# The squared decay of a gated recurrence, moved from a product on Pool to an exponential on ACT

## The reference, cut to what matters

```python
r = sigmoid(xb @ w_a + b_a)                     # (tokens, 1536)
ig = sigmoid(xb @ w_x + b_x)
log_a = -8.0 * r * softplus(-lam)               # lam: one value for each of the 1536 channels
a = exp(log_a)
bt = sqrt(-expm1(2.0 * log_a)) * (ig * xc)
hs = linear_scan(a, bt)                         # h_t = a_t * h_(t-1) + bt_t
y = hs * silu(g)
return y @ w_out                                # 1536 -> 1024
```

## Time and profile before

| | |
|---|---|
| median of 3 runs | 1854.46 us (1852.45 to 1854.9) |
| the profiled execution | 1852.57 us |
| its span, first to last instruction | 1850.8 us |
| PE busy | 1824.0 us, 99% of the span |
| DVE busy | 1047.5 us, 57% |
| ACT busy | 761.0 us, 41% |
| POOL busy | 208.9 us, 11% |
| recurrent layer with its output projection | from 1597.6 us on |

### The profile page before, as it was taken

How to read it: one execution, slowest core, us unless ns; L and a number is a source line. 1 busy time by engine, 2 the same in 40 slices (tenths; PEclk the granted TensorE clock), 3 DMA queues, 4 the chain that set the end, 5 groups by cost and what they waited for, 6 DMA issues and landing times.

```text
span 1850.8 us, 22596 instructions
## 1 busy us (share of the span) xinstructions
PE 1824.0 (99%) x8210; PEld 1461.3 (79%) x8210; DVE 1047.5 (57%) x1270; ACT 761.0 (41%) x1059; POOL 208.9 (11%) x175
## 2 busy tenths in 40 slices
PE   7999999999999999999999999999999999999997
PEld 5888888888766788888888878787787878788876
DVE  6444443343666665444443347766475566869973
ACT  5333332323544544333233345354343443456662
POOL 3000001011000002000001110100201102213343
PEclk9999999999999999999999999999999999999998
DMA  3232333344321132323223333232222222232333
GB/s 141 91 102 91 102 95 109 102 145 132 98 75 46 58 103 92 102 91 102 92 101 102 102 97 116 74 98 91 80 87 78 92 91 69 91 97 98 103 118 110
DMA packets 50304, 178.60 MB, mean 97 GB/s; under 512 B 5880, under 2 KB 6136, under 8 KB 50240
## 3 DMA queue, kind: packets, MB, share of 16 engines
q1 hardware_dynamic: 46512, 167.27, 27.6%
q0 software_dynamic: 2352, 8.15, 1.5%
q10 hardware_dynamic: 1376, 2.30, 0.3%
HBM read 173.48 MB, written 2.11 MB: 95 GB/s over the span
## 4 chain that ended last, share of the span: by engine, by line
PE 95%; DVE 2%; ACT 2%; POOL 1%; issue 1%; DMA 0%; POOLq 0%; ACTq 0%; DVEq 0%
PE banks L494 28%; PE banks L496 28%; PE banks L495 27%; PE banks L797 2%; PE banks L634 1%; PE banks L684 1%; PE banks L617 1%; PE banks L760 1%; PE banks L780 1%; PE banks L782 1%; PE banks L781 1%; DVE u_lo L1535 1%; ACT w_hi L1006 1%; DVE w_lo L1518 1%; POOL sumsq L2216 1%
## 5 line engine op out<-in xcount | busy, mean ns | idle before, releaser
L1518 DVE TENSOR_TENSOR w_lo<-w_raw,w_hi 128x1024 fp32r<-128x1024 f32 x315 | 403.2, 1280 | 593.2 <-ACT w_hi L1006 592.5
L494 PE MATMUL banks<-u_hi,w_hi 128*128 128x512 f32 x1528 | 607.4, 397 | 15.7 <-DVE u_lo L1535 15.6
L496 PE MATMUL banks<-u_hi,w_lo 128*128 128x512 f32 x1528 | 596.0, 390 | 0.0
L495 PE MATMUL banks<-u_lo,w_hi 128*128 128x512 f32 x1528 | 595.7, 390 | 0.0
L1006 ACT ACTIVATE w_hi<-w_raw 128x1024 fp32r<-128x1024 f32 x315 | 333.3, 1058 | 596.6 <-PE banks L496 551.4
L494 PEld LDWEIGHTS banks<-u_hi,w_hi 128*128 128x128 f32 x1528 | 287.2, 188 | 95.1 <-issue 16.5
L496 PEld LDWEIGHTS banks<-u_hi,w_lo 128*128 128x128 f32 x1528 | 287.4, 188 | 61.3
L495 PEld LDWEIGHTS banks<-u_lo,w_hi 128*128 128x128 f32 x1528 | 287.6, 188 | 60.8 <-issue 3.1
L495 PE MATMUL banks<-hid_lo,w_hi 128*128 128x512 f32 x352 | 136.9, 389 | 0.0
L496 PE MATMUL banks<-hid_hi,w_lo 128*128 128x512 f32 x352 | 136.9, 389 | 0.0
L494 PE MATMUL banks<-hid_hi,w_hi 128*128 128x512 f32 x352 | 136.9, 389 | 0.0
(11 more groups left out here) (290 smaller groups left out, 2329.3 us busy)
## 6 DMA issues: line engine op xcount, KB each, us to landing
w_raw<-weights SPq DMA_DIRECT2D x315, 512.0 KB, 3.5
bias<-neighbour_bias POOLq DMA_DIRECT2D x8, 384.0 KB, 4.9
x<-x_t ACTq DMA_DIRECT2D x4, 512.0 KB, 7.5
v_win<-v_a POOLq DMA_DIRECT2D x16, 128.0 KB, 5.3
out_t<-x SPq DMA_DIRECT2D x8, 256.0 KB, 2.3
nm<-gate_rows POOLq DMA_DIRECT2D x4, 256.0 KB, 3.8
fl<-gate_rows POOLq DMA_DIRECT2D x4, 256.0 KB, 3.4
rope<-rope_table POOLq DMA_DIRECT2D x1, 512.0 KB, 5.2
```

Of the source, the lines that this page charges most:

```text
L494: nc.tensor.matmul(o, wh, hi, start=start and k == 0, stop=False)
L495: nc.tensor.matmul(o, wh, lo, start=False, stop=False)
L496: ins = nc.tensor.matmul(o, wl, hi, start=False, stop=stop and k == len(pairs) - 1)
L1518: nc.vector.tensor_tensor(w_lo[:, n.slot, :], w_raw[:, n.slot, :], w_hi[:, n.slot, :].bitcast(F32), ALU.subtract)\
```

## The change

The square is no longer made by POOL. In `decay_tanh` ACT waits for its own Tanh, which must have read `rgate`, and then overwrites `rgate` with exp(-16 r s). Row 0 of `rate`, no longer needed once the softplus is made, takes the scale -16 s from one more small DVE instruction, and ACT waits for that one too before it goes on.

```diff
@@ decay_tanh(p, c), ACT
                 nc.scalar.activation(tanh[:, c, :], rgate[:, p % 2, c, :], ACT.Tanh, scale=rate[:, 4, 3 * p + c:3 * p + c + 1]).then_inc(r_act, 1)
+                act.wait_ge(r_act, 6 * p + 2 * c + 2)
+                nc.scalar.activation(rgate[:, p % 2, c, :], rgate[:, p % 2, c, :], ACT.Exp, scale=rate[:, 0, 3 * p + c:3 * p + c + 1])\
+                  .then_inc(a_squared, 1)
@@ ACT, group 0
-                    act.wait_ge(rate_dve, 3)
+                    act.wait_ge(rate_dve, 4)
@@ DVE, group 0
                     nc.vector.tensor_scalar(rates[4], rates[2], LRU_C, None, ALU.mult).then_inc(rate_dve, 1)
+                    nc.vector.tensor_scalar(rates[0], rates[2], -2.0 * LRU_C, None, ALU.mult).then_inc(rate_dve, 1)
@@ POOL, each group
-                for c in range(3):
-                    pool.wait_ge(r_act, 6 * p + 2 * c + 2)
-                    nc.gpsimd.tensor_tensor(rgate[:, p % 2, c, :], decay[:, c, :], decay[:, c, :], ALU.mult).then_inc(a_squared, 1)
```

## The result

The changed kernel takes 1856.36 us (median of 20 runs, 1855.19 to 1857.31) and the kernel before 1853.29 us (20 runs, 1852.08 to 1854.9): a ratio of 1.0016, with an interval of 1.001 to 1.0022. That is +3.1 us. These 20 runs of the kernel before have a median 1.17 us under that of the first three (1854.46 us), from which the forecast started. The profiled execution has a span of 1853.9 us against 1850.8 us, also +3.1 us.

A forecast was written before the change was run, and what follows sets the result against it. PE was taken to bound the kernel, waiting in group 3 for `w_lo` behind ACT's block. Three chunks at 0.75 us add 2.25 us, other terms 0: 1854.46 + 2.25 = 1856.7 us, range 1854.0 to 1859.4 us.

The forecast's parts named there:

- the likeliest case: Whole kernel: only ACT's longer chain in group 3 counts, +2.25 us to 1856.7 us; chance 0.67.
- The bound and the place: Group 3: PE waits 1.7 us for `w_lo` behind ACT's block; a delay there passes to the end in full.
- The cost of a chunk, 0.75 us: Group 3 on ACT: each new Exp costs 0.62 + 0.13 = 0.75 us, three chunks 2.25 us.
- The clock falls in the longer gap.: Rival, behind PE's gap in group 3: slower matmuls, +3.5 to +4.75 us in all, 1858.0 to 1859.2 us; chance 0.20.
- DVE is relieved: Rival, groups 0 to 2: without POOL's squares DVE gains 1.3 us each, -1.7 us in sum, 1852.8 us; chance 0.03.
- Nothing to win: 0: Removing POOL's twelve products, 14.5 us busy, gains 0, as nobody waits for them and PE has no wait for DVE there.
- Late units in groups 0 to 2: Rival: a chunk costing 1.8 us makes PE's units late there too, +9.6 us, 1864 us; chance 0.04.
- Cost 0: Groups 0 to 2: the new Exps are hidden; `w_hi` starts about 1660.35 us, DVE took it only at 1662.23 us.
- The sum.: Whole kernel: 1854.46 + 2.25 = 1856.7 us, +0.12%.

The follow-up runs named there:

- experiment 4: Changed kernel with group 3's three new Exps behind the next unit's `w_hi` instead of ahead of it: 1851.85 us, ratio 0.9994 to the kernel before.
- experiment 5: Changed kernel with only one chunk of group 3 squared on ACT, the other two on POOL: 1853.07 us, ratio 1.0 to the kernel before.
- experiment 6: Changed kernel with two chunks of group 3 squared on ACT, one on POOL: 1856.12 us, ratio 1.0012 to the kernel before.
- experiment 7: Changed kernel with group 3's new Exps behind all three Exp and Tanh pairs, still ahead of `w_hi`: 1855.13 us, ratio 1.0011 to the kernel before.
- Experiment 3: Changed kernel with 14 extra matmuls filling PE's gap in group 3: 1854.93 us, ratio 1.0007 to the kernel before.
- experiment 8: Changed kernel with only group 3's first Exp and Tanh ahead of `w_hi`, its square and two chunks behind: 1851.76 us, ratio 0.9991 to the kernel before.
- experiment 9: Changed kernel with group 3's ACT work spread over three places around the next units' `w_hi`, squares on ACT: 1851.69 us, ratio 0.9987 to the kernel before.
- experiment 10: Kernel before with group 3's ACT work spread over three places, squares still on POOL: 1851.33 us, ratio 0.9988 to the kernel before.
- experiment 1: Changed kernel with squares of groups 0 to 2 on ACT, those of group 3 on POOL: 1853.02 us, ratio 0.9995 to the kernel before.
- experiment 2: Changed kernel with squares of group 3 on ACT, those of groups 0 to 2 on POOL: 1856.87 us, ratio 1.0018 to the kernel before.

## Why the prediction was right in its range, and where its steps were not

The forecast of 1856.7 us is 0.3 us from the median, and that closeness is luck. The start was 1.17 us too high, since the median of three runs was 1854.46 us and that of 20 is 1853.29 us; the change was 0.8 us too small, +2.25 us for +3.1 us. Within the change two more errors partly cancelled: a loss of 1.57 us by the clock and a gain of 0.73 us were both left out of the likeliest case.

- **The bound and the place.** Right. Across the gap PE loses what ACT's chain grows by; what is behind it adds only the clock.
- **The cost of a chunk, 0.75 us.** Right: 0.74 us from Tanh to Exp where I had 0.75, and 0.75 to 0.76 us a chunk by experiments 4, 5, 6 and the changed kernel. Its two parts, 0.62 us of issue and 0.13 us of lost overlap and release, are shown by experiment 7, which takes the second away.
- **"The clock falls in the longer gap."** This was the rival with a chance of 0.20, and it is what the profile shows: 8 matmuls at 0.43 us, 1.57 us, inside the 1.25 to 2.5 us that I had priced. The rival's total of 1858.0 to 1859.2 us was not reached, because of the start and of the gain. Experiment 3 shows PE's idleness to be the cause. The rule of the Trainium skill (TensorE: Matmul & The Clock Gate, section HAM oscillation), that waits of PE between bursts bring the clock down, agrees with this trace. How often it falls is not shown, but the 20 times point to nearly always: the fastest is 1855.19 us, 3.11 us above the fastest of before (1852.08 us), where an execution without the fall would be expected near 1853.6 us. The runs lie in two clusters, seven from 1855.2 to 1855.7 us and ten from 1856.6 to 1857.3 us, with three between; the profiled execution, 1855.70 us with the fall behind the gap, is of the faster one, so the clusters do not tell executions with that fall from executions without it.
- **"DVE is relieved", chance 0.03.** Also there, at 0.73 us instead of my bound of 4.0 us. The step that failed is "Nothing to win: 0" under "What is removed", with its reason that PE has no wait for DVE in groups 0 to 2. I had read the list of PE's waits, which leaves out pauses of a few tenths. The distances between PE's starts show them, and so do the waits of the weight loads: `rc_lo` for the first gate unit was the operand that came last. SBUF — State Buffer (section Who interferes with whom) in the Trainium skill says why POOL's work slows DVE's, and the single rows of this trace agree (last section).
- **Late units in groups 0 to 2, and "Cost 0" there.** The units were not late, and the added Exps cost nothing: the `w_hi` that I put at 1660.35 us started at 1660.51 us in a trace that runs 0.15 us later, and DVE took it at 1661.83 us.
- **The sum.** With both: 2.29 + 1.57 - 0.73 = +3.13 us, and the small rest of -0.03 us. The likeliest case should have held the lower clock; its chance was too small. The wait of 1.66 us in one profile, at the full clock, was too little to build 0.67 on. The price of the clock was read from the earlier trace rows by the distance of 0.43 us alone; that this is the lower level is shown only by the windows of the changed kernel, where the same distance has a granted clock of 0.56 and 0.58 beside it.

Left open: why ACT's `w_hi` at 1772.53 us came 0.3 us later after PE's unit in each kernel with POOL's squares in groups 0 to 2. Its transfer was issued 6.6 us ahead of it before and 6.3 us after, and transfers land in 3.5 us, so the transfer is not the cause. This is 0.3 of the 0.73 us, so for that part the runs show only that it goes with POOL's squares, not how. Also open is whether the wait of 1.7 us costs the kernel before its clock in some executions; the gain of versions 8 to 10 may hold some of that.

## What to carry to other kernels

Moving work from an idle engine to a busy one costs by its place: the same three instructions cost 3.9 us ahead of the copy that PE waited for (pieces B and C of the changed kernel) and nothing behind it (experiment 4), so find first which instruction the next unit waits for, and put new work after it. Price a wait of PE with the clock that it may lose, not by its own length alone. And before writing "no wait, so nothing to gain", look at the distances between PE's starts and at the waits of the weight loads: a pause that hides in the overlap of two matmuls is not in the list of PE's waits.

## What the runs showed of the hardware that I had not expected

**The clock fell after rather short waits.** In group 3 it stayed at the full level behind the wait of 1.7 us in all three traces that have it (before, experiments 1 and 4), and fell at or soon after the wait in all five with 2.43 us or more (changed, 2, 5, 6 and 7). In experiment 5 it fell after 2.43 us of idle PE, more than 1 us after PE had begun again; in experiment 1, whose group 3 was undisturbed, it fell at another place, after the 1.90 us for `u_lo` ahead of the recurrent layer:

```profile
1604.43 0.67 PE L494 MATMUL banks<-u_hi,w_hi 128*128 128x512 f32 x1 [1.90 <-DVE u_lo L1539]
1604.90 0.63 PE L495 MATMUL banks<-u_lo,w_hi 128*128 128x512 f32 x1
```

while the changed kernel passed the same wait at the full clock:

```profile
1604.56 0.50 PE L494 MATMUL banks<-u_hi,w_hi 128*128 128x512 f32 x1 [1.85 <-DVE u_lo L1538]
1604.89 0.40 PE L495 MATMUL banks<-u_lo,w_hi 128*128 128x512 f32 x1
```

That wait lasts 1.85 to 1.90 us in all twelve traces, and the clock fell within 1.5 us after it in five (experiments 1, 3, 5, 8 and 9), so its length does not decide. The matmul at which piece A begins stands at 1639.33 us in experiment 1 and at 1637.86 us in the changed kernel: 1.5 us between two executions of a part that is nearly the same in both kernels. That is about half of the spread of 2 to 3 us between runs, so a difference of 1 us has to be read in pieces of the trace.

**A DVE instruction with two inputs in SBUF and a POOL product hold each other up, both ways.** The rows of the kernel before one by one, where the earlier trace rows have three L1589 in a single row:

```profile
1657.02 1.31 POOL L2315 TENSOR_TENSOR rgate<-decay 128x512 f32<-128x512 f32 x1 [1.13 <-ACT tanh L1413]
1657.47 1.41 DVE L1589 SCALAR_TENSOR_TENSOR rc<-xr,vecs,rc 128x512 f32<-128x512 f32 x1
1658.30 1.48 POOL L2315 TENSOR_TENSOR rgate<-decay 128x512 f32<-128x512 f32 x1
1658.92 1.41 DVE L1589 SCALAR_TENSOR_TENSOR rc<-xr,vecs,rc 128x512 f32<-128x512 f32 x1
```

Alone, L1589 takes 0.75 us (three in 2.33 us) and the square 1.04 us. Each of the last three rows ends 0.55 to 0.90 us after the row above it has ended, so each did most of its work only when the other engine's instruction was over.
